# Low halves of a weight unit made by GpSimd in four pieces of 256 columns, each with its own count

## What is computed

```python
def first_block(x, ...):
    h = rmsnorm(x, ln1_g[l]);  proj = h @ w_in[l]
    ...
    mix = jax.nn.sigmoid(ga) * (oa @ w_branch_a[l]) + jax.nn.sigmoid(gb) * (ob @ w_branch_b[l])
    x = x + mix @ w_out[l]
    h2 = rmsnorm(x, ln2_g[l])
    x = x + jnp.square(jax.nn.relu(h2 @ w_up[l])) @ w_down[l]

def second_block(x, ...):
    for l in range(DEPTH_2):
        x = x + 0.5 * _swiglu(_rms_norm(x, ffn1_norm[l]), ffn1_wi[l], ffn1_wo[l])
        u = _rms_norm(x, mix_norm[l]);  c = _split_cols(u @ w_in[l] + b_in[l])
        ...
        merged = (g[:, :, 0] * (y_sb @ w_up_sb[l]) + g[:, :, 1] * (y_ml @ w_up_ml[l])
                  + g[:, :, 2] * (y_mla @ w_up_mla[l]))
        x = x + merged @ w_out[l]
        x = x + 0.5 * _swiglu(_rms_norm(x, ffn2_norm[l]), ffn2_wi[l], ffn2_wo[l])
```

## Time and profile before

| | |
|---|---|
| median of 3 runs | 2593.98 us (2593.46 to 2594.09) |
| the profiled execution | 2592.74 us |
| its span, first to last instruction | 2590.9 us |
| TensorE busy | 2512.7 us, 97% |
| VectorE busy | 1404.5 us, 54% |
| ScalarE busy | 938.3 us, 36% |
| GpSimd busy | 994.9 us, 38% |
| mean granted TensorE clock | 0.987 of 2.4 GHz |
| DMA engines busy | 27% |

### The profile page before, as it was taken

How to read it: one execution, slowest core, us unless ns; L and a number is a source line. 1 busy time by engine, 2 the same in 40 slices (tenths; PEclk the granted TensorE clock), 3 DMA queues, 4 the chain that set the end, 5 groups by cost and what they waited for, 6 DMA issues and landing times.

```text
span 2590.9 us, 27957 instructions
## 1 busy us (share of the span) xinstructions
PE 2512.7 (97%) x11206; PEld 1994.8 (77%) x11206; DVE 1404.5 (54%) x1972; ACT 938.3 (36%) x1495; POOL 994.9 (38%) x432
## 2 busy tenths in 40 slices
PE   7999999999999999999899999999999889999999
PEld 7777767888888888666677788888886666777887
DVE  5768667644335642359744754444324696358441
ACT  4444443322223222533533442332335353244321
POOL 3423224444444444233323444444431342334443
PEclk9999999999999999999999999999999899999999
DMA  4211112333333333112122333333331211223333
GB/s 169 78 34 56 49 58 90 98 96 93 96 98 110 97 94 101 49 49 65 49 66 82 93 95 98 98 96 94 95 95 41 63 60 44 79 81 97 91 97 98
DMA packets 59601, 213.30 MB, mean 82 GB/s; under 512 B 6608, under 2 KB 6736, under 8 KB 59344
## 3 DMA queue, kind: packets, MB, share of 16 engines
q1 hardware_dynamic: 59472, 211.52, 26.9%
HBM read 209.39 MB, written 2.10 MB: 82 GB/s over the span
## 4 chain that ended last, share of the span: by engine, by line
PE 82%; DVE 13%; issue 2%; ACT 1%; POOL 1%; DMA 0%; SPq 0%; DVEq 0%; ACTq 0%; POOLq 0%
PE banks L659 81%; DVE t L1359 1%; DVE t L1499 1%; DVE t L1496 1%; DVE t L999 1%; DVE t L1092 1%; DVE t L1001 1%; DVE t L1195 1%; DVE t L1501 1%; POOL t L1793 1%; DVE t L997 1%; DVE t L1401 1%; DVE t L1098 0%; PE banks L768 0%; ACT t L1542 0%
## 5 line engine op out<-in xcount | busy, mean ns | idle before, releaser
L659 PE MATMUL banks<-t,t 128*128 128x512 f32 (+7 forms) x10854 | 2478.6, 392 | 56.4 <-POOL t L1793 24.7
L659 PEld LDWEIGHTS banks<-t,t 128*128 128x128 f32 (+2 forms) x10854 | 1956.4, 190 | 544.3 <-issue 89.4
L1793 POOL TENSOR_TENSOR t<-t,t 128x1024 fp32r<-128x1024 f32 x387 | 939.2, 2427 | 1514.5 <-ACT t L1542 1514.5
L1542 ACT ACTIVATE t<-t 128x1024 fp32r<-128x1024 f32 x387 | 409.7, 1059 | 1179.6 <-PE banks L659 1177.1
L1092 DVE TENSOR_TENSOR t<-banks,t 128x512 f32<-128x512 f32 x121 | 83.4, 689 | 222.1 <-PE banks L659 221.9
L981 DVE SCALAR_TENSOR_TENSOR t<-t,t,t 128x512 fp32r<-128x512 f32 x64 | 113.9, 1780 | 62.4 <-ACT t L1551 62.4
L1252 DVE TENSOR_TENSOR t<-banks,t 128x512 f32<-128x512 f32 x44 | 30.4, 691 | 180.6 <-PE banks L659 180.4
L1195 DVE CAST t<-t 128x512 fp32r<-128x512 f32 x68 | 116.5, 1713 | 2.4
L1220 DVE SCALAR_TENSOR_TENSOR t<-banks,t 128x512 f32<-128x512 f32 x32 | 22.1, 692 | 153.1 <-PE banks L659 153.1
L1239 DVE CAST t<-t 128x512 fp32r<-128x512 f32 x32 | 67.7, 2115 | 30.5 <-ACT t L1657 30.5
L1801 POOL TENSOR_TENSOR t<-t,t 128x512 f32<-128x512 f32 x33 | 47.3, 1432 | 70.5 <-DVE t L1001 70.5
(11 more groups left out here) (160 smaller groups left out, 1305.3 us busy)
## 6 DMA issues: line engine op xcount, KB each, us to landing
t<-in_w SPq DMA_DIRECT2D x387, 512.0 KB, 3.5
t<-in_xT SPq DMA_DIRECT2D x8, 256.0 KB, 6.4
out<-t SPq DMA_DIRECT2D x8, 256.0 KB, 4.4
t<-in_dmask SPq DMA_DIRECT2D x1, 1536.0 KB, 11.9
t<-in_vbias SPq DMA_DIRECT2D x2, 384.0 KB, 4.1
t<-in_c SPq DMA_DIRECT2D x1, 576.0 KB, 8.5
t<-in_pos SPq DMA_DIRECT2D x2, 256.0 KB, 6.7
t<-in_smask SPq DMA_DIRECT2D x1, 256.0 KB, 12.1
```

Of the source, the lines that this page charges most:

```text
L659: return pe.matmul(o, l, r, start=start, stop=stop, skip_group_check=True)
L1542: a.activation(whl[u % 2][:, 0:1024], wraw[u % 3][:, :], ACT.Copy).then_inc(*w_high.next(u))
L1793: p.tensor_tensor(hl[:, 1024:2048], wraw[u % 3][:, :], as_f32(hl[:, 0:1024]), ALU.subtract).then_inc(*w_low.next(u))
```

## The change

GpSimd makes the low half in four instructions of 256 columns, two blocks each, one after the other, and each counts up `w_low` under a name of its own, (u, q). TensorE waits, before block i of unit u, for quarter i // 2; a wide group of blocks waits for the quarter of its last block. ScalarE, before it writes over a buffer, waits for the last quarter of unit u - 2 beside TensorE's end with that unit. SyncE's load waits for the last quarter of unit u - 3. The planner's costs stand as they are; it now prices four short instructions where it priced one.

```diff
             def weights(n):
                 u, i = divmod(n, 8)
                 hl = whl[u % 2]
-                need.wait_ge(*w_low.at(u))
+                need.wait_ge(*w_low.at((u, i // 2)))
                 return hl[:, 128 * i:128 * i + 128], hl[:, 1024 + 128 * i:1152 + 128 * i]
@@ wide
-                weights(ns[0])
+                weights(ns[-1])
@@ ScalarE, half_weights
                 if u >= 2:
                     need.wait_ge(*t_dense.at(("unit", u - 2)))
+                    need.wait_ge(*w_low.at((u - 2, 3)))
                 a.activation(whl[u % 2][:, 0:1024], wraw[u % 3][:, :], ACT.Copy).then_inc(*w_high.next(u))
@@ GpSimd, half_weights
                 hl = whl[u % 2]
-                p.tensor_tensor(hl[:, 1024:2048], wraw[u % 3][:, :], as_f32(hl[:, 0:1024]),
-                                ALU.subtract).then_inc(*w_low.next(u))
+                for q in range(4):
+                    c = slice(256 * q, 256 * q + 256)
+                    p.tensor_tensor(hl[:, 1024:2048][:, c], wraw[u % 3][:, c], as_f32(hl[:, c]),
+                                    ALU.subtract).then_inc(*w_low.next((u, q)))
@@ SyncE, load_weights
                 if u >= 3:
-                    need.wait_ge(*w_low.at(u - 3))
+                    need.wait_ge(*w_low.at((u - 3, 3)))
                 sp.dma_start(wraw[u % 3][:, :], w[u]).then_inc(*in_w[u % 3].next(u))
```

## The result

The changed kernel takes 2553.8 us (median of 5 runs), the kernel before 2594.0 beside it: ratio 0.9849, 95% interval 0.9838 to 0.986, 40.2 us faster. The forecast was 2564, 30 us faster.

The account below looks back on a forecast made before the run. TensorE, busy 2512.7 of 2590.9 us, was taken as the bound. From 2592.7 us profiled, 24 for waits and 6 for the clock gave 2562.7; with the runs' median 1.2 above, 2564, range 2540 to 2596.

Parts of the forecast that it names:

- The piece: GpSimd's 256-column subtraction: 0.74 us for the first, 0.69 for each next, 2.8 us a unit instead of 2.4.
- Part 1: TensorE's waits for GpSimd's low halves: a block needs only its own quarter, which comes sooner; 11.8 us less.
- the sign given for this part: In the profile after, TensorE's waits for L1793 near 13 us, of which 9.3 before the first matmul.
- Part 2: VectorE's SBUF instructions before TensorE's waits: held for one piece, at most 0.74 us; 28 us, the larger part.
- the discount: On the 39.8 us of TensorE's shortened single waits: 0.6 kept, 24 us, bounds 12 and 38, as VectorE may be no earlier.
- The maximum of L1001: Sign for VectorE's held instruction in the profile after: near 1.3 us instead of 2.77.
- Part 3: TensorE's granted clock, low behind idle spots that the change shortens: 6 us, bounds 17 and -3.
- Part 4: About 1160 more waits on TensorE and other added costs: 0; steady matmuls stay at 225.6 ns each.
- Part 5: The planner's order of steps, shifted by its new price for the subtraction: 0, with 8 us on both sides.
- rival C: The planner's new order puts TensorE steps before their inputs are ready: slower, 2605 us, chance 0.12.
- B: VectorE's SBUF instructions come in stacks, each held by its own piece; only early quarters gain, 11 us: 2583, chance 0.17.

Follow-up runs that it names:

- e1: Four pieces, but TensorE waits for the unit's last piece, every step in the order of the kernel before; 2552.5 us, ratio 0.9845 to the kernel before.
- e3: The changed kernel with its four pieces and counts, but every step in the order of the kernel before; 2551.5 us, ratio 0.9845 to the kernel before.
- e2: The changed kernel's order of steps, but the low half in one GpSimd instruction again; 2588.3 us, ratio 0.9982 to the kernel before.
- e8: Four pieces in the 196 feed-forward units only, one instruction elsewhere, order of the kernel before; 2596.8 us, ratio 1.0011 to the kernel before.
- e11: Four pieces in the 191 other units only, one instruction in the feed-forward units, order of the kernel before; 2554.8 us, ratio 0.9853.
- e10: The changed kernel with eight pieces of 128 columns and the head products moved to VectorE, an order of its own; 2549.8 us, ratio 0.9842.
- e7: The kernel before, but GpSimd subtracts only 128 of 1024 columns from the third unit on, part of the computation left out; 2517.3 us, ratio 0.9705.
- e5: The change with two pieces of 512 columns, every step in the order of the kernel before; 2572.0 us, ratio 0.9917 to the kernel before.
- e4: The change with two pieces of 512 columns, in an order of its own; 2566.2 us, ratio 0.9896 to the kernel before.
- e6: The change with eight pieces of 128 columns, every step in the order of the kernel before; 2549.1 us, ratio 0.9824 to the kernel before.

## Why the prediction was right, and where it wasn't

**The piece.** Forecast 0.74 us, measured 0.743 in the median; a unit in a row 2.8. In the mean a piece takes 0.845, as VectorE's instructions get in between, and GpSimd's busy time grew by 321 us, not by the 155 forecast. Right for a piece that nothing disturbs.

**Part 1, early quarters.** Forecast 11.8 us. The waits themselves shrank nearly as worked out, by 10.4 from e1 to e3, but the kernel got 1 us from it, which is within the noise. (In the order of the change they shrank by only 6.7, to 18.0 us, and the sign given for this part was 13.) The step that failed is the sum over single waits: TensorE reached the next place sooner, where VectorE or a head product was no earlier. The text had said that such waits come back and kept 0.6 of everything; for this part it should have kept nothing. That four pieces put the head product 0.4 us and more further back was named, and priced at 0: e3 shows 5.4 us of waits for it, 0.7 before. It isn't the pieces alone: e1 has them too and waits 0.9 us for it, since its TensorE comes later.

**Part 2, short holds.** Forecast 28 us before the discount, 17 after it. e1 has this part alone: TensorE idles 28.3 us less, while GpSimd's own waits grew by 1.9. So the 28 was right in sum and the discount wrong. The lists of before and after alone would have said the opposite: 6.7 and 19.1 us went, close to the discounted 7 and 17. Only e1 shows that the short holds bring all of the idle time without the early quarters. Line by line, before against after, the forecast holds only in part: L1001 lost 8.6 us of waits (5.0 forecast), L1401 all 9.0 (8.8), L1197 3.3 (2.6), L1092 2.8 (4.4), L1327 0.8 (3.2), and two grew by the new order, L1176 by 3.3 and L997 by 3.0, as e2 has 6.1 and 4.3 for them. The mechanism is shown three times: by the timeline at 1139, by e1, and by e8 and e11, which say where it counts. The maximum of L1001 was to be 1.3 us and is 1.67. The row at 1189.85 explains it, a head product is in the way and not a piece:

```profile
1189.49 1.47 POOL L1804 TENSOR_TENSOR t<-t,t 128x512 f32<-128x512 f32 x1
1189.85 1.67 DVE L1001 TENSOR_TENSOR t<-t,t 128x512 f32<-128x512 f32 x1
```

**Part 3, the clock.** Forecast 6 us, measured 12.0 in busy time and 13.3 by the mean clock. This term was the mis-sized one, half of what was measured. In the idle time two errors met: the discount on part 2 was too large, and what part 1 was to bring did not come. The sum of the two was forecast as 24 us and measured as 27.3, and that these lie so near is luck. 27.3 and 12.0 make the 39.3 us of the span. Busy time isn't the clock alone, though: e1 was granted 0.995, which by the same sum is worth 20.9 us, and its busy time fell by 11.9. What makes the difference isn't shown.

**Part 4, the added waits.** Forecast 0. The two windows of 610 us have the same 2723 matmuls, and the long chain of pure matmuls, which was to stay at 225.6 ns each, has 225.0:

```profile
399.79 655.71 PE banks L659 x2914
```

Right.

**Part 5, the order.** Forecast 0 within 8. -5 us with one instruction, 0 with four. Right within its bounds, and rival C is out: the new order costs nothing, with one piece or with four. That holds for this order. In e10's, two waits of 9.5 us stand where an instruction was placed six units later.

**The rivals.** B, holds in stacks, is true where it was placed, but it doesn't decide the time: it allowed 11 us, all from the early quarters, and e1 gains 40 without them. After, the four SBUF instructions in a row at the end of a merge are each held by a piece, and GpSimd's four take 3.90 us; TensorE still waits for the last of them:

```profile
1453.11 3.90 POOL L1796 TENSOR_TENSOR t<-t,t 128x256 fp32r<-128x256 f32 x4 [1.08 <-ACT t L1543]
1453.15 1.25 DVE L1499 TENSOR_TENSOR t<-t,t 128x512 f32<-128x512 f32 x1
1454.43 1.11 DVE L1501 TENSOR_TENSOR t<-t,t 128x512 f32<-128x512 f32 x1
1455.58 0.84 DVE L1195 CAST t<-t 128x512 fp32r<-128x512 f32 x1
1456.46 1.10 DVE L1197 TENSOR_TENSOR t<-t,t 128x512 fp32r<-128x512 f32 x1
...
1457.62 0.73 PE L659 MATMUL banks<-t,t 128*128 128x512 f32 x2 [0.92 <-DVE t L1197]
```

Before, the same wait was longer:

```profile
1483.19 1.20 PE L659 MATMUL banks<-t,t 128*128 128x512 f32 x4 [1.35 <-DVE t L1197]
```

So 0.4 us of it went, where the forecast had left some 0.3, (2.6 - 2.1) / 2. The Trainium skill (page SBUF — State Buffer, section "Who interferes with whom") says that the shared port pair is locked for a whole instruction and that issue order decides who blocks. These rows agree: the two engines take turns, instruction by instruction, and GpSimd's four take 3.90 us instead of 2.8.

**What stays open:** how the 34 us between four pieces and e7 split into remaining holds, later low halves and clock; whether the clock's share follows idle time in any simple way; and what else is in TensorE's busy time. e1 and e3 differ by 1.2 us in idle time and by 2.0 in busy time, the other way round.

## What to carry to other kernels

A long GpSimd instruction on SBUF costs most where VectorE has one short instruction to do before TensorE can go on; look for VectorE instructions that take several times their usual length and end a fixed time after GpSimd's (0.54 us for L1001 here), and count only those in front of a wait of TensorE. Cut it into pieces: at about four times the fixed cost of 0.19 us (256 columns) the gain of cutting was nearly complete here (41.6 of 44.3 us), though far from what a shorter instruction altogether gives. An operand that is ready sooner shortens the wait for it, and that is only a gain if what TensorE needs next is ready sooner too: here 10 us of waits went and 1 us of time, within the noise. Before such a gain is forecast, add up what a list of waits gives, but don't take the list as proof: here it gave 6.7 us to a part that brought nothing to be seen.

## What the runs showed of the hardware

- GpSimd's subtraction is a straight line from 128 to 1024 columns: 0.463, 0.743, 1.298 and 2.4 us.
- GpSimd and VectorE take turns at instruction ends, so VectorE's busy time falls with each halving: 1404.5, 1366.0, 1225.4, 1138.9 us. The first halving brought only 38 us, the second 141. That comes from instructions in pairs. Before, the first of a pair takes the whole hold and the second runs free; with two pieces each is held by a piece of its own. L1195 and L1197, which follow each other, before (first) and in e5, busy and mean ns:

```profile
L1195 DVE CAST t<-t 128x512 fp32r<-128x512 f32 x68 | 116.5, 1713 | 2.4
...
L1197 DVE TENSOR_TENSOR t<-t,t 128x512 fp32r<-128x512 f32 x68 | 51.2, 753 | 2.3
```

```profile
L1197 DVE TENSOR_TENSOR t<-t,t 128x512 fp32r<-128x512 f32 x68 | 88.8, 1305 | 2.3
...
L1195 DVE CAST t<-t 128x512 fp32r<-128x512 f32 x68 | 72.7, 1069 | 2.4
```

  The pair takes 2.47 us before, 2.37 with two pieces and 1.87 with four (0.815 and 1.053 in e3). That is rival B's mechanism, in VectorE's busy time.
- Some 1160 more waits on TensorE cost nothing that 2723 matmuls show.
- The granted clock differs between executions of one kernel as well as between kernels. In e4 it went from 0.994 to 0.987 and the time from 2557.0 to 2574.3 us. Between before (0.987) and e7 (0.997) TensorE's busy time for the same matmuls fell from 2512.7 to 2487.3 us. Busy time follows the mean clock only roughly: e6 and e10 both had 0.990, with 2506.4 and 2494.5 us.
